# 28 instead of 24 seven-product pairs in a two-layer transformer kernel, with the modulation pieces moved around them

## The chip, the core and the metric

The kernel runs on one core of one Trainium2 chip. A core has TensorE (PE, matrix products into PSUM), VectorE (DVE), ScalarE (ACT), GpSimd (POOL) and SyncE (SP); each works through its own instructions in order, and they wait for each other by semaphores. The metric is the device time of one execution in microseconds (us), lower is better.

## The reference

Two layers over 256 latent and 256 context tokens of width 1024. Each layer has a gated feed-forward part (FFN), a mixer (differential attention, a short gated convolution, a multi-scale pool) and a second FFN; in the second layer that last FFN runs on the latent tokens alone. Every part is normalised, scaled and shifted by modulation vectors, and its result is gated by one:

```python
mod = (silu_c @ w_mod[l] + b_mod[l]).reshape(B, N_MOD, D_MODEL)
mod_c = (silu_cc @ w_mod[l] + b_mod[l]).reshape(1, N_MOD, D_MODEL)
h = h + 0.5 * m[2][:, None] * _swiglu(_modulate(_rms(h, norm_w[l, 0]), m[0], m[1]),
                                      ffn1_w_gu[l], ffn1_w_down[l])
...
y, yc = _hybrid_mixer(u, uc, ctx_out, w_in[l], w_out[l], ...)
h = h + m[5][:, None] * y
h = h + 0.5 * m[8][:, None] * _swiglu(_modulate(_rms(h, norm_w[l, 2]), m[6], m[7]),
                                      ffn2_w_gu[l], ffn2_w_down[l])

def _swiglu(x, w_gu, w_down):
    g, u = jnp.split(x @ w_gu, 2, axis=-1)
    return (jax.nn.silu(g) * u) @ w_down
```

All of it is in float32; the FFN's inner width is 2816.

## The kernel before

**Numbers.** A float32 value is held as a high and a low part, and a product is three matmuls: high x high, high x low, low x high (`three`, lines 1741 to 1743). For the weights ACT makes the high part `whi` (line 575, a "split" below) and DVE the low part `wlo` (line 1023) of each block of 128 x 1024 weights that SP loads into `raw`, a ring of five blocks; SP loads a block when the one five before it is done.

**The FFNs.** They are numbered by `f`: 0 and 1 in the first layer, 2 and 3 in the second; called FFN 0 to FFN 3 below. An FFN has 22 pairs `j` of blocks (gate and up, 256 x 2 token columns) and then two down halves of 11 blocks. A plain pair is 2 x 8 x 3 = 48 matmuls of 512 columns. ACT takes SiLU of the gate (line 588) and DVE multiplies it with up (`hidden`, line 1055).

**Seven-product pairs.** For some pairs (`SEVENS[f]`) the 2 x 2 block product of (gate, up halves) and (token halves) is made with seven products instead of eight: 7 x 4 x 3 = 84 matmuls of 256 columns (`seven_products`). This needs, once per FFN, four sums of the token halves: DVE writes them in pairs 1 and 2 (`x_whole`, `x_sums`: `t32`), ACT makes the high parts `thi` (line 602) and DVE the low parts `tlo` (line 1098, four instructions in pair 3). And it needs, for each such pair, sums of the weight halves: `weight_sums` on DVE (lines 1110 to 1115), `shi` on ACT (line 613), `slo` on DVE (line 1121). PE's order in such a pair: two products of plain parts, then one with `tlo` (it waits for all four), then one that waits for ACT's copy of the pair's first product (`first_copy`, line 622), then three with the weight sums. DVE adds the results up in `seven_begin` (lines 1141, 1145) and `seven_end` (lines 1155, 1157), ACT takes SiLU in two parts (lines 630, 633), `seven_mul` (line 1166) multiplies. `SECOND[f]` names pairs whose weight sums and PSUM banks are a second set; it is empty before.

**Modulation.** The modulation vectors are made beside the FFNs, in 36 units of four pieces (`mod_pair`, line 1041): GpSimd loads a piece of 512 KB into one of two buffers `wm` when the one before is used, and DVE multiplies and accumulates it with the conditioning vector, once per stream (from unit `X_ONLY` = 28 on, for the latent tokens alone). `UNIT_AT[f]` says which units an FFN makes, `MODS_GU[f]` how many pieces stand in each pair, ahead of that pair's `hidden`, and `MODS_DN[f]` how many in each down block.

The order on each engine is that of the code, written out by hand: these tables set it. The functions that the change touches:

Of the kernel before, what the change touches and what calls it, by code (L numbers as in the profile page):

```python
# [64 lines left out]
PAIRS = DC // 2  # L65
# [57 lines left out]
def program(nc, wstream, wmod, cols, x_t, out):  # L123
    with ExitStack() as ctx:
# [394 lines left out]
        def _(pool):  # L519
# [37 lines left out]
            loads(u0 // 2 + 1, after_mix)  # L557
            zeros(0)
            conv_pool_low(0)
            loads(after_mix, UNITS * PAIRS // 2)  # L560
            zeros(1)
            conv_pool_low(1)


        @block.scalar
        def _(act):
# [212 lines left out]
            def mixer(l):  # L779
# [229 lines left out]
        def _(dve):  # L1009
# [21 lines left out]
            def mod_pair(u, p, junk=products):  # L1031
# [337 lines left out]
            def ffn_last():  # L1369
# [1004 lines left out]
```

## Time and profile before

| | us |
|---|---|
| median of 3 runs | 1620.0 (1619.54 to 1620.85) |
| profiled execution, its time | 1619.6 |
| profiled execution, its span | 1617.9 |
| FFN 1, pairs 4 to 20 of its gate/up part | 628 to 806 of the span |
| FFN 2, pairs 4 to 20 | 985 to 1163 |
| FFN 3 | 1404 to 1615 |

All times below are microseconds from the span's start. In the rows, a line of a timeline has start, duration (from the first start to the last end where instructions are merged, x2), engine, line of the code, operation, result<-operands and sizes, and in brackets how long the engine was idle before it and what ended that. Neighbouring instructions overlap by about 0.08 us in these records, so the step from one start to the next is the time one takes in a row of them. The granted clock (PEclk) is the share of TensorE's 2.4 GHz.

### The profile page before, as it was taken

What the parts mean: (1) busy time and instruction counts of PE and PEld (TensorE: products, weight loads), DVE (VectorE), ACT (ScalarE), POOL (GpSimd) and SP (SyncE); (2) the same over time, 40 slices, a digit from 0 to 9 for tenths busy, and PEclk for the clock granted to TensorE, in tenths of its full rate; (3) what the DMA queues carried; (4) which work ended last, traced back from release to release, by engine and by line L of the source; (5) the groups of instructions that cost most, each with busy time, mean ns of one, the idle gap of its engine ahead of it and who ended that gap; (6) DMA issues with size and microseconds to landing.
All of it is one profiled execution on the core that took longest, in us unless ns stands there. A gap on an engine that the chain in (4) does not pass through costs nothing.

```text
span 1617.9 us, 24542 instructions
## 1 busy us (share of the span) xinstructions
PE 1607.8 (99%) x9540; PEld 1407.4 (87%) x9540; DVE 1257.3 (78%) x1926; ACT 697.3 (43%) x1068; POOL 84.6 (5%) x149
## 2 busy tenths in 40 slices
PE   8999999999999999999999999999999999999999
PEld 4889898889878898999988898999988997999888
DVE  5889887888878678788878788888766587887654
ACT  5433233324856454333333154333333275665542
POOL 0000000100000100000000000001000000100000
PEclk9999999999999999999999999999999999999999
DMA  9455554663321223344445434445645332355554
GB/s 378 152 195 176 175 178 149 194 196 105 109 75 53 79 92 118 132 168 156 170 142 189 165 111 133 144 155 200 208 159 205 125 111 82 113 197 182 184 190 148
DMA packets 69615, 250.48 MB, mean 155 GB/s; under 512 B 7552, under 2 KB 8576, under 8 KB 69376
## 3 DMA queue, kind: packets, MB, share of 16 engines
q1 hardware_dynamic: 51072, 181.84, 33.5%
q0 software_dynamic: 18432, 67.12, 11.9%
q8 instruction: 75, 1.23, 0.3%
q14 instruction: 36, 0.29, 0.1%
HBM read 247.88 MB, written 1.05 MB: 154 GB/s over the span
## 4 chain that ended last, share of the span: by engine, by line
PE 95%; DVE 2%; DMA 1%; ACT 1%; issue 0%; DVEq 0%; ACTq 0%
PE ps L1741 28%; PE ps L1742 28%; PE ps L1743 28%; PE ps L1784 3%; PE ps L1832 2%; PE ps L1785 2%; PE ps L1834 1%; PE ps L2153 1%; PE ps L1893 1%; PE ps L2121 1%; DMA raw<-wstream 1%; PE ps L2135 0%; DVE nmax L1548 0%; PE ps L1863 0%; DVE shared_b L1219 0%
## 5 line engine op out<-in xcount | busy, mean ns | idle before, releaser
L1023 DVE TENSOR_TENSOR wlo<-raw,whi 128x1024 fp32r<-128x1024 f32 x320 | 386.6, 1222 | 203.9 <-ACT whi L575 201.3
L1741 PE MATMUL ps<-xh,whi 128*128 128x512 f32 (+1 forms) x1388 | 481.2, 347 | 2.9 <-DVE xl L1227 2.3
L575 ACT ACTIVATE whi<-raw 128x1024 fp32r<-128x1024 f32 x320 | 335.1, 1055 | 341.4 <-PE ps L1743 254.8
L1742 PE MATMUL ps<-xl,whi 128*128 128x512 f32 (+1 forms) x1388 | 473.3, 341 | 0.0
L1743 PE MATMUL ps<-xh,wlo 128*128 128x512 f32 (+1 forms) x1388 | 472.9, 341 | 0.0
L1741 PEld LDWEIGHTS ps<-xh,whi 128*128 128x128 f32 x1388 | 262.8, 189 | 38.9 <-DVE xl L1227 4.4
L1742 PEld LDWEIGHTS ps<-xl,whi 128*128 128x128 f32 x1388 | 263.1, 190 | 29.8 <-issue 0.7
L1743 PEld LDWEIGHTS ps<-xh,wlo 128*128 128x128 f32 x1388 | 262.8, 189 | 30.0
L1742 PE MATMUL ps<-al,whi 128*128 128x512 f32 (+2 forms) x768 | 263.1, 343 | 0.0
L1741 PE MATMUL ps<-ah,whi 128*128 128x512 f32 (+1 forms) x668 | 235.3, 352 | 0.0
L1743 PE MATMUL ps<-ah,wlo 128*128 128x512 f32 (+1 forms) x668 | 234.8, 351 | 0.0
L1742 PEld LDWEIGHTS ps<-al,whi 128*128 128x128 f32 x768 | 145.5, 190 | 17.0
L1741 PEld LDWEIGHTS ps<-ah,whi 128*128 128x128 f32 x668 | 126.2, 189 | 18.1
L1743 PEld LDWEIGHTS ps<-ah,wlo 128*128 128x128 f32 x668 | 126.3, 189 | 16.8
L530 POOL DMA_DIRECT2D wm<-wmod x126 | 66.6, 528 | 991.0 <-DVEq L1045 982.4
L1041 DVE SCALAR_TENSOR_TENSOR wm<-wm,cb 128x1024 f32<-128x1024 f32 x96 | 117.1, 1220 | 0.0
L588 ACT ACTIVATE shared_b<-ps 128x512 f32<-128x512 f32 x42 | 25.1, 598 | 195.5 <-PE ps L1743 195.4
L1041 DVE SCALAR_TENSOR_TENSOR shared_a<-wm,cb 128x1024 f32<-128x1024 f32 x73 | 89.1, 1221 | 11.4 <-DMA wm<-wmod 7.1
L1784 PE MATMUL ps<-xh,whi 128*128 128x512 f32 x208 | 73.5, 399 | 0.0
L1041 DVE SCALAR_TENSOR_TENSOR shared_b<-wm,cb 128x1024 f32<-128x1024 f32 x55 | 67.0, 1218 | 4.8 <-DMA wm<-wmod 4.6
L630 ACT ACTIVATE shared_b<-shared_a 128x256 f32<-128x256 f32 x24 | 10.0, 417 | 135.3 <-DVE shared_a L1141 135.3
L741 ACT ACTIVATE shared_a<-h 128x256 f32<-128x256 f32 (+1 forms) x64 | 31.4, 496 | 66.9 <-DVE h L1177 64.3
(218 smaller groups left out, 2442.6 us busy)
## 6 DMA issues: line engine op xcount, KB each, us to landing
raw<-wstream SPq DMA_DIRECT2D x320, 512.0 KB, 3.5
wm<-wmod POOLq DMA_DIRECT2D x128, 512.0 KB, 4.8
wm<-wmod SPq DMA_DIRECT2D x8, 1024.0 KB, 17.0
h<-x_t SPq DMA_DIRECT2D x4, 512.0 KB, 6.8
cb<-cols SPq DMA_DIRECT2D x1, 1024.0 KB, 19.1
out_t<-h SPq DMA_DIRECT2D x8, 128.0 KB, 2.5
K<-cols SPq DMA_DIRECT2D x1, 907.0 KB, 19.6
K<-cols SPq DMA_DIRECT2D x1, 265.5 KB, 2.9
```

Source lines behind the costliest of these rows:

```text
L530: pool.dma_start(wm[:, c, :, :].rearrange("p a n -> p (a n)"), wmod[bass.ds(i * 2 + c, 1)].rearrange("a p n -> p (a n)"))\
L575: act.activation(whi[:, n % SPL, :, :].rearrange("p a b -> p (a b)"), raw[:, n % RING, :], ACT.Copy)\
L588: act.activation(sil[:, j % 2, 0:w], ps[:, gu_bank(f, 2 * j), 0:w], ACT.Silu).then_inc(silu_done, 1)
L741: act.activation(sq[:, d % 2, a:b], h[:, d, a:b], ACT.Square).then_inc(sq_done, 1)
L1023: dve.tensor_tensor(wlo[:, n % RING, :, :].rearrange("p a b -> p (a b)"), raw[:, n % RING, :], whi[:, n % SPL, :, :].rearrange("p a b -> p ...
L1041: dve.scalar_tensor_tensor(rows if v else junk, rows, 1.0, cb[:, v, :], ALU.mult, ALU.mult, accum_out=flat[:, at:at + 1])\
L1741: pe.matmul(out_ap, hi_w, hi_x, start=start, stop=False)
L1742: pe.matmul(out_ap, hi_w, lo_x, start=False, stop=False)
L1743: return pe.matmul(out_ap, lo_w, hi_x, start=False, stop=stop)
L1784: pe.matmul(ps[:, bank, :], whi[:, n % SPL, c, :], xh[:, c, :], start=c == 0, stop=False)
L1785: return pe.matmul(ps[:, bank, 0:S], wlo[:, n % RING, c, :], xh[:, c, 0:S], start=False, stop=c == DC - 1)
L1832: pe.matmul(ps[:, banks[d], 0:2 * w], hi_w, pair.rearrange("p v t -> p (v t)"), start=start, stop=False)
```

## The change

`SEVENS[1]` and `SEVENS[2]` go from nine to eleven pairs: 4, then runs of two (6 and 7, 9 and 10, 12 and 13, 15 and 16), then 18 and 20. Pairs 7, 10, 13 and 15 use the second set of sums and banks. The modulation pieces of these two FFNs move: one each in pairs 1, 2 and 3, two in the plain pairs 5, 8, 11, 14, 17 and 19, one in 16, 18 and 20. FFN 2 makes 9 units instead of 11; the last two (the gate of FFN 3) are made in FFN 3, one piece per block in the first eight blocks of its first down half, and the gate's columns behind them. GpSimd's loads of those come behind its mixer work. FFN 0 is as it was.

```diff
-UNIT_AT = {0: (4, 12), 1: (16, 9), 2: (25, 11)}
+UNIT_AT = {0: (4, 12), 1: (16, 9), 2: (25, 9), 3: (34, 2)}
...
-          (4, 6, 8, 10, 12, 14, 16, 18, 20),
-          (4, 6, 8, 10, 12, 14, 16, 18, 20))
+          (4, 6, 7, 9, 10, 12, 13, 15, 16, 18, 20),
+          (4, 6, 7, 9, 10, 12, 13, 15, 16, 18, 20))
...
-           {1: 1, 5: 1, 7: 2, 9: 2, 10: 1, 11: 1, 12: 1, 13: 1, 14: 1, 15: 2, 17: 2, 19: 2, 20: 1},
+           {1: 1, 2: 1, 3: 1, 5: 2, 8: 2, 11: 2, 14: 2, 16: 1, 17: 2, 18: 1, 19: 2, 20: 1},
...
-SECOND = ((), (), ())
+SECOND = ((), (7, 10, 13, 15), (7, 10, 13, 15))
...
-            loads(after_mix, UNITS * PAIRS // 2)
+            after_gu = UNIT_AT[3][0] * PAIRS // 2 + 1
+            loads(after_mix, after_gu)
             zeros(1)
             conv_pool_low(1)
+            loads(after_gu, UNITS * PAIRS // 2)
...
-                    act.wait_ge(mod_col, UNITS)
+                    act.wait_ge(mod_col, UNIT_AT[3][0])
...
-                    dve.scalar_tensor_tensor(rows if v else junk, rows, 1.0, cb[:, v, :], ALU.mult, ALU.mult,
+                    dve.scalar_tensor_tensor(junk if u < X_ONLY and v == 0 else rows, rows, 1.0, cb[:, v, :], ALU.mult, ALU.mult,
...
-                gate_columns(m)
...
+                u0, nu = UNIT_AT[f]
                 for b in range(HALF):
                     split_next(nd + b)
+                    if b < nu * PAIRS:
+                        mod_pair(u0 + b // PAIRS, b % PAIRS)
+                mod_columns(u0, nu)
+                gate_columns(m)
```

The table for FFN 2 becomes the same as that for FFN 1. The order that this gives, in the built programs (in the changed one most lines have moved by two):

On DVE, FFN 1, from the last token sums of pair 2 to behind the low parts `tlo` in pair 3 (`hid<-shared_b,ps` is `hidden`, `s` the weight sums, `wlo` a split, `wm` a modulation piece). Before:

```order
L1089 SCALAR_TENSOR_TENSOR t<-t,hid 128x1024
L1092 SCALAR_TENSOR_TENSOR t<-t,hid 128x1024
L1055 TENSOR_TENSOR hid<-shared_b,ps 128x512
L1110 TENSOR_TENSOR s<-raw 128x512
L1111 TENSOR_TENSOR raw<-raw 128x512
L1113 TENSOR_TENSOR s<-s,raw 128x512
L1115 TENSOR_TENSOR s<-s,raw 128x512
L1023 TENSOR_TENSOR wlo<-raw,whi 128x1024 x2
L1121 TENSOR_TENSOR slo<-s,shi 128x1536
L1098 TENSOR_TENSOR tlo<-t,thi 128x1024 x4
L1055 TENSOR_TENSOR hid<-shared_b,ps 128x512
```

and on DVE at the same place now:

```order
L1094 SCALAR_TENSOR_TENSOR t<-t,hid 128x1024
L1043 SCALAR_TENSOR_TENSOR shared_a,modc<-wm,cb 128x1024
L1043 SCALAR_TENSOR_TENSOR wm,modc<-wm,cb 128x1024
L1057 TENSOR_TENSOR hid<-shared_b,ps 128x512
L1112 TENSOR_TENSOR s<-raw 128x512
L1113 TENSOR_TENSOR raw<-raw 128x512
L1115 TENSOR_TENSOR s<-s,raw 128x512
L1117 TENSOR_TENSOR s<-s,raw 128x512
L1025 TENSOR_TENSOR wlo<-raw,whi 128x1024 x2
L1123 TENSOR_TENSOR slo<-s,shi 128x1536
L1100 TENSOR_TENSOR tlo<-t,thi 128x1024 x4
L1043 SCALAR_TENSOR_TENSOR shared_a,modc<-wm,cb 128x1024
```

A piece (two instructions) now stands ahead of pair 2's `hidden`, and one more behind `tlo`.

On ACT, FFN 1, a seven-product pair and the one behind it (`shared_b<-ps 128x256` is the first copy, the two lines `128x2x128` the SiLU parts, `whi` a split, `shi` the sums). Before, pairs 4 to 6:

```order
L622 ACTIVATE shared_b<-ps 128x256
L630 ACTIVATE shared_b<-shared_a 128x2x128
L633 ACTIVATE shared_b<-shared_b 128x2x128
L575 ACTIVATE whi<-raw 128x1024 x2
L613 ACTIVATE shi<-s 128x1536
L588 ACTIVATE shared_b<-ps 128x512
L575 ACTIVATE whi<-raw 128x1024 x2
L622 ACTIVATE shared_b<-ps 128x256
```

and on ACT the run of pairs 6 and 7 now:

```order
L624 ACTIVATE shared_b<-ps 128x256
L577 ACTIVATE whi<-raw 128x1024 x2
L615 ACTIVATE shi_more<-s_more 128x1536
L632 ACTIVATE shared_b<-shared_a 128x2x128
L635 ACTIVATE shared_b<-shared_b 128x2x128
L577 ACTIVATE whi<-raw 128x1024 x2
L624 ACTIVATE shared_b<-ps 128x256
```

The first copy of a run's second pair now stands behind both SiLU parts of the first pair and two splits.

On DVE, the first down half of FFN 3. Before:

```order
L1402 TENSOR_TENSOR shared_b<-shared_b 128x256
L1065 TENSOR_TENSOR ah<-shared_b,ah 128x256
L1023 TENSOR_TENSOR wlo<-raw,whi 128x1024 x11
L1184 SCALAR_TENSOR_TENSOR h<-ps,gcol,h 128x256
L1186 SCALAR_TENSOR_TENSOR h<-ps,gcol,h 128x256
```

and on DVE the end of that half now:

```order
L1025 TENSOR_TENSOR wlo<-raw,whi 128x1024
L1043 SCALAR_TENSOR_TENSOR wm,modc<-wm,cb 128x1024
L1025 TENSOR_TENSOR wlo<-raw,whi 128x1024 x3
L1052 TENSOR_TENSOR modc<-modc,K 128x16
L1173 TENSOR_SCALAR gcol<-modc 128x16
L1186 SCALAR_TENSOR_TENSOR h<-ps,gcol,h 128x256
```

A one-instruction piece stands behind each of the first eight splits, and the gate's columns ahead of the first update.

## Rows read from the trace of the kernel before

**Rows 1.** The page: busy time of each engine.

```profile
PE 1607.8 (99%) x9540; PEld 1407.4 (87%) x9540; DVE 1257.3 (78%) x1926; ACT 697.3 (43%) x1068; POOL 84.6 (5%) x149
```

**Rows 2.** The page: the chain that ended last, by engine.

```profile
PE 95%; DVE 2%; DMA 1%; ACT 1%; issue 0%; DVEq 0%; ACTq 0%
```

**Rows 3.** Waits of PE: us in total, times, longest us.

```profile
PE ps L1741 <- DVE xl L1227: 2.3, 4, 0.6
```

**Rows 4.** Windows, FFN 1: us, PE, PEld, DVE, ACT, POOL busy, PEclk, DMA share, GB/s.

```profile
617.35:628.23 10.88, 10.88 (x49) 9.01 (x48) 10.78 (x12) 7.89 (x8) 0.00 (x0) 1.00 0.30 98
628.23:638.30 10.07, 10.07 (x85) 10.07 (x84) 6.71 (x8) 3.18 (x5) 0.00 (x0) 1.00 0.47 156
638.30:649.21 10.91, 10.91 (x50) 9.02 (x49) 10.35 (x14) 3.92 (x4) 0.00 (x0) 1.00 0.15 50
640.00:915.00 275.00, 275.00 (x1531) 241.42 (x1530) 223.54 (x316) 94.07 (x121) 17.43 (x33) 1.00 0.48 161
```

**Rows 5.** Timeline of DVE, FFN 1, pairs 1 to 3: start, us, what.

```profile
609.60 1.22 DVE L1041 SCALAR_TENSOR_TENSOR shared_a<-wm,cb 128x1024 f32<-128x1024 f32 x1
...
612.47 0.69 DVE L1055 TENSOR_TENSOR hid<-shared_b,ps 128x512 f32<-128x512 f32 x1 [0.50 <-DVE wm L1041]
...
618.88 0.68 DVE L1055 TENSOR_TENSOR hid<-shared_b,ps 128x512 f32<-128x512 f32 x1
619.47 0.68 DVE L1110 TENSOR_TENSOR s<-raw 128x512 f32<-128x512 f32 x1
...
622.12 2.36 DVE L1023 TENSOR_TENSOR wlo<-raw,whi 128x1024 fp32r<-128x1024 f32 x2
624.40 1.75 DVE L1121 TENSOR_TENSOR slo<-s,shi 128x1536 fp32r<-128x1536 f32 x1
626.07 4.62 DVE L1098 TENSOR_TENSOR tlo<-t,thi 128x1024 fp32r<-128x1024 f32 x4
```

**Rows 6.** Timelines: first matmul with the token sums (FFN 1); the same place in FFN 2.

```profile
631.10 0.28 PE L1741 MATMUL ps<-thi,whi 128*128 128x256 f32 x1
...
982.50 4.62 DVE L1098 TENSOR_TENSOR tlo<-t,thi 128x1024 fp32r<-128x1024 f32 x4
...
984.70 0.28 PE L1741 MATMUL ps<-xh,whi 128*128 128x256 f32 x1
```

**Rows 7.** Timeline of DVE, FFN 1, pair 7: two pieces, then the hidden product.

```profile
667.56 1.22 DVE L1041 SCALAR_TENSOR_TENSOR shared_a<-wm,cb 128x1024 f32<-128x1024 f32 x1
...
670.08 1.23 DVE L1041 SCALAR_TENSOR_TENSOR shared_a<-wm,cb 128x1024 f32<-128x1024 f32 x1
...
672.60 0.69 DVE L1055 TENSOR_TENSOR hid<-shared_b,ps 128x512 f32<-128x512 f32 x1
```

**Rows 8.** Timelines of DVE and ACT, FFN 1: sums, SiLU, splits, first copy.

```profile
805.12 0.69 DVE L1141 TENSOR_TENSOR shared_a<-shared_b,ps 128x512 f32<-128x512 f32 x1 [0.25 <-DVE wm L1041]
...
807.02 0.42 ACT L633 ACTIVATE shared_b<-shared_b 128x256 f32<-128x256 f32 x1 [0.70 <-DVE shared_b L1155]
...
670.88 2.00 ACT L575 ACTIVATE whi<-raw 128x1024 fp32r<-128x1024 f32 x2
672.78 0.38 ACT L622 ACTIVATE shared_b<-ps 128x256 f32<-128x256 f32 x1
```

**Rows 9.** FFN 3's first down split on DVE; the page's issue row of the pieces.

```profile
1557.77 1.22 DVE L1023 TENSOR_TENSOR wlo<-raw,whi 128x1024 fp32r<-128x1024 f32 x1 [1.00 <-ACT whi L575]
...
wm<-wmod POOLq DMA_DIRECT2D x128, 512.0 KB, 4.8
```

**Rows 10.** PE's opening groups (3.8 to 8.9, 9.8 to 14.2); windows at the end.

```profile
L1893 PE MATMUL ps<-K 128*128 128x512 f32 x6 | 5.5, 1088 | 3.8 <-DMA K<-cols 3.8
...
L1893 PE MATMUL ps<-K 128*128 128x512 f32 x11 | 4.9, 593 | 0.0
...
1614.85:1616.85 2.00, 0.17 (x2) 0.00 (x0) 0.77 (x2) 0.00 (x0) 0.00 (x0) 1.00 0.64 214
1616.95:1617.90 0.95, 0.00 (x0) 0.00 (x0) 0.00 (x0) 0.00 (x0) 0.00 (x0) 0.50 0.14 45
```

More of the change, by code:

```diff
@@ L83 @@
 SEVENS = ((7, 9, 11, 14, 17, 19),
-          (4, 6, 8, 10, 12, 14, 16, 18, 20),
-          (4, 6, 8, 10, 12, 14, 16, 18, 20))
+          (4, 6, 7, 9, 10, 12, 13, 15, 16, 18, 20),
+          (4, 6, 7, 9, 10, 12, 13, 15, 16, 18, 20))
 MODS_GU = ({2: 1, 3: 1, 4: 2, 5: 2, 6: 2, 8: 2, 9: 1, 10: 2, 11: 1, 12: 2, 13: 2, 14: 1, 15: 2, 16: 2, 18: 2, 19: 2, 20: 2},
-           {1: 1, 5: 1, 7: 2, 9: 2, 10: 1, 11: 1, 12: 1, 13: 1, 14: 1, 15: 2, 17: 2, 19: 2, 20: 1},
-           {1: 1, 5: 1, 6: 1, 7: 2, 9: 2, 11: 2, 12: 1, 13: 2, 14: 2, 15: 2, 16: 2, 17: 2, 18: 2, 19: 2, 20: 2})
+           {1: 1, 2: 1, 3: 1, 5: 2, 8: 2, 11: 2, 14: 2, 16: 1, 17: 2, 18: 1, 19: 2, 20: 1},
+           {1: 1, 2: 1, 3: 1, 5: 2, 8: 2, 11: 2, 14: 2, 16: 1, 17: 2, 18: 1, 19: 2, 20: 1})
 MODS_DN = ({0: 1, 1: 1, 2: 1, 3: 1, 4: 1, 5: 1, 6: 1, 7: 1, 8: 1, 9: 1, 10: 1, 11: 1, 12: 2, 13: 1, 14: 1, 15: 1, 16: 1, 17: 1},
```

## The prediction

> **What bounds the kernel now.** I read the page's busy line first: TensorE (PE) is busy 99% of the span, VectorE (DVE) 78%, ScalarE (ACT) 43% [rows 1]. PE's busy time alone proves little, so the chain of work that ended last comes next: 95% of it is PE [rows 2]. Then who waited for whom on PE: the longest group behind the first load is four waits of at most 0.6 us at stage boundaries [rows 3], and none lies inside the gate/up part of FFN 1 or 2. The windows over single pairs show the same from inside: PE is busy 10.88 of 10.88 us, 10.07 of 10.07, 10.91 of 10.91, and 275.00 of 275.00 over the rest of FFN 1 [rows 4]. So there PE's work is the time: what it loses in work is won, and every wait it gets is paid in full. DVE in the pair before the first seven-product pair is busy 10.78 of 10.88 us [rows 4]: it has no room exactly where that pair's operands are made.
>
> **Part 1, the pairs that become seven-product.** A plain pair is 48 matmuls and lasts 10.88 us, or 10.91 right behind a seven-product pair; a seven-product pair is 84 shorter ones and lasts 10.07 [rows 4]. FFN 1 and FFN 2 go from 9 to 11 such pairs each. Two pairs become shorter: 2 x (10.88 - 10.07) = 1.62 us. The runs of two leave 7 instead of 9 plain pairs behind a seven-product pair: 2 x 0.03 = 0.06. Each FFN gains 1.68 us, the two 3.36. All of it is on the path, because PE waits for nothing there [rows 4].
>
> **Part 2, the piece that moves into pair 2.** A modulation piece is two multiply-accumulates on DVE. One follows the other every 2.52 us (670.08 to 672.60) [rows 7]; once 2.87 us passed (609.60 to 612.47) [rows 5]. Before, pair 1 holds one and pairs 2 to 4 none; now pairs 1, 2 and 3 hold one each. In pair 2 the piece stands ahead of the hidden product, and behind it on DVE stand that product, the weight sums, two splits, the low part of the sums, and the four low parts of the token sums (tlo). In the trace these run without a gap from 618.88 on and tlo ends at 626.07 + 4.62 = 630.69 [rows 5]. The first seven-product pair of FFN 1 starts at 628.23, and its third product, the first that reads tlo, at 631.10 [rows 4, 6]. The slack is 0.41 us, some 0.37 after a handover of about 0.04. A piece more pushes tlo by 2.52: PE would wait 2.52 - 0.37 = 2.15 us. ACT's part moves along, since its sums wait for the same DVE instructions. FFN 2 has the same picture: tlo ends at 982.50 + 4.62 = 987.12, the pair starts at 984.70 and wants tlo 2.88 later, at 987.58; slack 0.42, wait 2.52 - 0.42 + 0.04 = 2.14 [rows 6]. Together +4.28 us. From both sides: nothing, if DVE found a gap to put the piece in, which the rows exclude; 2 x (2.87 - 0.37) = 5.0 with the slow piece. I take 4.28, since nearly all pieces go at 2.52. The piece in pair 3 stands behind tlo and delays only the hidden product of pair 3 (0.6) and the two splits of pair 5 (2.28): 633.2 + 2.52 + 0.6 + 2.28 = 638.6, and PE, itself 2.15 late, reaches pair 5 at 638.30 + 2.15 = 640.45. It costs nothing.
>
> **Part 3, the runs of two.** Here ACT becomes tight. The copy of a pair's first product, for which PE's fourth product waits, now stands in the second pair of a run behind the first pair's second SiLU and two splits. I queue it up from rows. In the trace pair 7 is a plain pair with two pieces, behind a seven-product pair, as the plain pair ahead of a run will be. It starts at 628.23 + 10.07 + 10.91 + 10.07 = 659.28, its pieces at 667.56, its hidden product at 672.60, and DVE is free at 673.2, which is 3.0 us into the next pair (670.19) [rows 4, 7]. In a run of two, DVE then makes the second pair's weight sums (619.47 to 622.12, 2.65), two splits (2.28) and the low part (1.67) [rows 5]: 9.6. From the first sum of the gate to ACT's second SiLU is 805.12 to 807.02, 1.90; that SiLU takes 0.32, two splits 1.90, the copy 0.38 [rows 8]: 14.1 us after the run began, 14.2 with handovers. PE wants it at 10.07 + 3/7 x 10.07 = 14.39. It fits by 0.2 us, in each of the eight runs. I cost it at nothing. If DVE is later than that by more than 0.2, each run pays the excess.
>
> **Part 4, the last gate's units.** FFN 2 loses eight pieces that were hidden there. FFN 3 gets eight, one multiply of 1.2 us each, between the splits of its first down half. There DVE splits a block every 2.8 us, about four blocks ahead of PE (1557.77 for a block that PE reaches some 9 us later) [rows 9]. Two pieces lie ready; six come by DMA, 4.8 us to land [rows 9] plus issue and use, about 7.1 for two, or 21 for six, in the 17 us that PE spends on six blocks. DVE falls back by about 4 of its 9 us. Cost: nothing, unless landing grows beyond some 6.3 us; at 7 about 2 us. On GpSimd's queue the last loads move behind the mixer's work, which has long ended by then. The gate columns (0.2 us) are made on DVE before the sum that needs them.
>
> **Part 5, what the wait does to the clock.** Elsewhere PE waits 0.6 us at most and the granted clock stays at 1.00 (2.4 GHz) [rows 3, 4]. A wait of 2.15 us has no row before the end of the span. There PE is all but idle from 1614.85 on, the clock is still 1.00 up to 1616.85 and reads 0.50 (1.2 GHz) in the last microsecond [rows 10]. So two microseconds of quiet were enough once, and 2.15 us is as long as that. At the lower level PE does half its work: in the opening the first six matmuls took 1088 ns, the later ones 593, and the low stretch was 5.5 us of work [rows 10], so a fall costs between 0 and 2.7 us. I take the middle, 1.4.
> The Trainium skill ("TensorE: Matmul & The Clock Gate", section "HAM oscillation — how this bites in real kernels") says that idle gaps bring PE back to the lower level, but puts the gap that does so above the one worked out here. By that rule the clock holds and the sum is the first rival's 1620.9; the end of this trace speaks against leaning on it.
>
> **The sum.** Against the profiled execution (span 1617.9, time 1619.6): -3.36 + 4.28 = +0.9, and +1.4 for one fall of the clock out of two waits: 1621.9. The median of the runs shown is 1620.0, 0.4 above the profiled one, so for a median **1622.3**. A measurement of this kernel can tell about 0.2% (3.2 us) from no change, so this is "no change": the gain of four pairs goes into two waits for tlo.
>
> **The rivals.** First, the clock holds through both waits: 1620.0 + 0.9 = 1620.9. For it: 1.00 in every earlier stretch; against it: no wait there is as long. Second, on the slower side, the clock falls at both waits and stays low as long as in the opening: 0.9 + 2 x 2.7 = +6.3, 1626.3. It decides for "slower" from (3.2 - 0.9) / 2 = 1.2 us a fall. Third, the runs: with two slow pieces of 2.87 in the plain pair DVE is 0.7 later, the copy comes 0.5 late, eight times: +4.0, 1624.9 with the clock held. Only one such piece is in the rows. Fourth, the wait for tlo doesn't come, because DVE finds the time: 1620.0 - 3.4 = 1616.6, just faster. The missing gap in [rows 5] speaks against it. Fifth, the DMAs of FFN 3 land late: 1620.9 + 2 = 1622.9.
>
> **How the numbers follow.** One fall 0.35, none 0.32, both 0.16, the runs 0.07, no wait 0.06, late DMAs 0.04. Slower by over 0.2% are both falls and the runs, 0.23; faster the fourth rival, 0.06; within 0.2% the rest, 0.71. The range takes in none to two falls and part of the rivals above: low 1619.0 (the clock held, less the scatter of the runs), high 1625.2.
>
> **What would show it.** Right: in PE's waits a new line, DVE tlo, two times, about 2.1 us each, in the first seven-product pair of FFN 1 and FFN 2; tlo ends 2.5 us later against that pair's start; seven-product pairs still 10.07; granted clock below 1.00 right behind one of the two waits. Wrong: no such wait (then 1616.6), waits of PE for ACT's first copy in the runs' second pairs, waits of PE for wlo in FFN 3's down half, or seven-product pairs longer than 10.07.

## The result: no change that counts, by two waits, a clock and one gain not forecast

| | us |
|---|---|
| kernel before, median of 20 runs | 1619.98 (1618.3 to 1621.85) |
| changed kernel, median of 20 runs | 1622.13 (1618.78 to 1626.37) |
| ratio, 95% interval | 1.0018 (1.0012 to 1.0024) |
| changed kernel, profiled execution: time, span | 1625.34, 1623.3 |
| changed kernel, a second profiled execution: span | 1619.5 |

The forecast was 1622.3, in a range of 1619.0 to 1625.2. The median is 2.1 us above the kernel before, where +2.3 was forecast, and the scatter is new: 7.6 us from the lowest run to the highest, against 3.6. That is why two executions of the changed kernel are read below; the first one is 3.2 us above the changed kernel's median, the second near it. In the rows, line numbers of DVE and ACT are 2 higher than before, those of PE 6 higher (in kernels with moved pieces in FFN 3 another 1 to 3).

The page's busy line and its chain, answering to [rows 1, 2]:

```profile
PE 1606.7 (99%) x9684; PEld 1413.9 (87%) x9684; DVE 1284.6 (79%) x1963; ACT 706.5 (44%) x1080; POOL 85.0 (5%) x149
...
PE 89%; DVE 7%; DMA 3%; issue 1%; ACT 1%; DVEq 0%; POOLq 0%; ACTq 0%
```

PE is busy 1.1 us less than before while the span is 5.4 us longer, and 7% of the chain is now DVE: PE has begun to wait. For whom, the waits of PE say (us in total, times, longest us); the last row was there before [rows 3], and so was the load at the start, left out here:

```profile
PE ps L1747 <- DVE tlo L1100: 5.6, 2, 2.8
PE ps L1838 <- DVE wlo L1025: 1.2, 1, 1.2
PE ps L1747 <- DVE xl L1229: 2.3, 4, 0.6
```

The windows over single pairs, answering to [rows 4] (us, PE, PEld, DVE, ACT, POOL busy, PEclk, DMA share, GB/s): pairs 3 and 4 of FFN 1, its run 6 and 7, pair 8, then pair 4 of FFN 2:

```profile
616.57:627.46 10.89, 10.89 (x50) 9.01 (x48) 10.64 (x14) 5.53 (x6) 0.53 (x1) 1.00 0.44 150
627.46:640.52 13.06, 10.29 (x85) 10.12 (x84) 12.18 (x14) 5.42 (x8) 0.53 (x1) 1.00 0.44 152
651.43:671.58 20.15, 20.15 (x169) 20.15 (x168) 16.22 (x21) 7.89 (x11) 1.06 (x2) 1.00 0.52 183
671.58:682.49 10.91, 10.91 (x51) 9.02 (x49) 10.46 (x15) 3.93 (x4) 0.00 (x0) 1.00 0.15 50
...
985.12:1000.83 15.71, 12.90 (x86) 12.72 (x84) 12.33 (x14) 5.47 (x8) 0.53 (x1) 0.78 0.42 134
```

A run of two lasts 20.15, twice 10.07, with PE busy throughout: the new pairs are as short as they should be. The loss of FFN 1 and FFN 2 sits in the two pairs 4, which last 3.0 and 5.6 us longer than a seven-product pair; the second also shows a granted clock of 0.78.

Where the time goes, stage by stage. A stage begins at the same matmul in each kernel: FFN 1 and FFN 2 at the first one behind PE's wait for xl. The other two are cut behind a pair of sums for the norms that stands in every kernel's order (line 1982 before): "mixer 2" begins within FFN 2's last blocks and takes in the first 29 us of FFN 3, "FFN 3" is the rest. The differences to the kernel before add up to that of the span:

| stage | before, us | changed | second execution |
|---|---|---|---|
| start to FFN 1 | 591.90 | -0.76 | -0.81 |
| FFN 1 | 356.49 | +1.18 | +0.84 |
| FFN 2 | 337.99 | +4.00 | +2.32 |
| mixer 2 | 145.13 | -0.85 | -0.76 |
| FFN 3 | 186.39 | +1.83 | +0.01 |
| span | 1617.90 | +5.40 | +1.60 |

FFN 1 and FFN 2 should each be 1.68 shorter for two new pairs; the waits and the clock make them longer. FFN 3's 1.83 holds the wait for wlo, 1.2. The first row is scatter: in the profiles of this study, with either kernel's opening, FFN 1 begins between 590.7 and 592.0. Mixer 2 is a gain that the prediction didn't have.

### The profile page after: what moved, and what is told of

It reads as the page before. It is cut to its first block, busy times and chain, and to the rows that moved or that the text cites. A ratio compares the mean times of both kernels' runs of the same rounds, so it can differ in the third digit from the quotient of the medians.

```text
span 1623.3 us, 24912 instructions
## 1 busy us (share of the span) xinstructions
PE 1606.7 (99%) x9684; PEld 1413.9 (87%) x9684; DVE 1284.6 (79%) x1963; ACT 706.5 (44%) x1080; POOL 85.0 (5%) x149
## 4 chain that ended last, share of the span: by engine, by line
PE 89%; DVE 7%; DMA 3%; issue 1%; ACT 1%; DVEq 0%; POOLq 0%; ACTq 0%
PE ps L1747 27%; PE ps L1748 26%; PE ps L1749 26%; PE ps L1790 3%; PE ps L1791 1%; DMA raw<-wstream 1%; DVE wlo L1025 1%; DMA wm<-wmod 1%; PE ps L2159 1%; DVE wm L1043 1%; PE ps L2127 1%; PE ps L1899 1%; PE ps L1838 1%; DVE tlo L1100 1%; DVE hid L1073 1%
## 5 line engine op out<-in xcount | busy, mean ns | idle before, releaser
L1747 PE MATMUL ps<-xh,whi 128*128 128x512 f32 (+1 forms) x1356 | 465.4, 343 | 2.7 <-DVE xl L1229 2.3
L1748 PE MATMUL ps<-xl,whi 128*128 128x512 f32 (+1 forms) x1356 | 457.5, 337 | 0.0
L1749 PE MATMUL ps<-xh,wlo 128*128 128x512 f32 (+1 forms) x1356 | 457.1, 337 | 0.0
L1747 PEld LDWEIGHTS ps<-xh,whi 128*128 128x128 f32 x1356 | 256.9, 189 | 36.0 <-DVE xl L1229 4.4
L1748 PEld LDWEIGHTS ps<-xl,whi 128*128 128x128 f32 x1356 | 257.1, 190 | 27.3 <-issue 0.7
L1749 PEld LDWEIGHTS ps<-xh,wlo 128*128 128x128 f32 x1356 | 256.9, 189 | 27.5
L1043 DVE SCALAR_TENSOR_TENSOR wm<-wm,cb 128x1024 f32<-128x1024 f32 x128 | 156.2, 1220 | 8.1 <-DMA wm<-wmod 7.4
L1043 DVE SCALAR_TENSOR_TENSOR shared_a<-wm,cb 128x1024 f32<-128x1024 f32 x59 | 72.0, 1221 | 4.1 <-DMA wm<-wmod 1.0
L1747 PE MATMUL ps<-thi,whi 128*128 128x256 f32 x224 | 64.7, 289 | 5.6 <-DVE tlo L1100 5.6
L1749 PE MATMUL ps<-thi,wlo 128*128 128x256 f32 x224 | 64.4, 288 | 0.0
```

The lines of the kernel that those rows point to most:

```text
L1043: dve.scalar_tensor_tensor(junk if u < X_ONLY and v == 0 else rows, rows, 1.0, cb[:, v, :], ALU.mult, ALU.mult, accum_out=flat[:, at:at + 1])\
L1747: pe.matmul(out_ap, hi_w, hi_x, start=start, stop=False)
L1748: pe.matmul(out_ap, hi_w, lo_x, start=False, stop=False)
L1749: return pe.matmul(out_ap, lo_w, hi_x, start=False, stop=stop)
```

## Why the wait is longer than forecast, and why it varies

DVE in pairs 2 to 4 of FFN 1 and PE in pair 4 (timelines: start, us, what), answering to [rows 5, 6]:

```profile
618.76 1.22 DVE L1043 SCALAR_TENSOR_TENSOR shared_a<-wm,cb 128x1024 f32<-128x1024 f32 x1
...
621.28 0.69 DVE L1057 TENSOR_TENSOR hid<-shared_b,ps 128x512 f32<-128x512 f32 x1
...
628.48 4.63 DVE L1100 TENSOR_TENSOR tlo<-t,thi 128x1024 fp32r<-128x1024 f32 x4
...
630.21 0.28 PE L1749 MATMUL ps<-xh,wlo 128*128 128x256 f32 x1
633.25 0.36 PE L1747 MATMUL ps<-thi,whi 128*128 128x256 f32 x1 [2.77 <-DVE tlo L1100]
```

The piece takes the forecast 2.52 us (618.76 to 621.28) and stands where it was expected. But the wait is 2.8, not 2.15. The missing 0.6 was lost 14 us ahead of the piece, when DVE began the sums of x. ACT's split of block 6 and DVE's first sum, in the changed kernel, then the same two in the kernel before:

```profile
602.71 1.06 ACT L577 ACTIVATE whi<-raw 128x1024 fp32r<-128x1024 f32 x1 [1.00 <-DMA raw<-wstream]
604.94 3.49 DVE L1073 TENSOR_TENSOR hid<-xh,xl 128x1024 f32<-128x1024 f32 x3
```

```profile
602.82 1.06 ACT L575 ACTIVATE whi<-raw 128x1024 fp32r<-128x1024 f32 x1 [0.20 <-DMA raw<-wstream]
605.06 1.22 DVE L1071 TENSOR_TENSOR hid<-xh,xl 128x1024 f32<-128x1024 f32 x1
```

PE began block 3 at 600.23 in the changed kernel and at 601.00 before, so DVE's first sum came 4.71 behind that instead of 4.06. Behind it DVE runs nearly without a gap, so the delay d of that first sum decides tlo. In the kernel before, tlo was in time by 0.37 at d = 4.06 in FFN 1, and by 0.38 at d = 4.36 in FFN 2 (where no slow piece stands ahead). So PE's wait should be 2.52 for each piece more in pair 2, plus d, less 4.43 in FFN 1 and less 4.74 in FFN 2. The executions in which PE waited for tlo with at most one piece more and no filler (the kernels are those of the experiments below), with d read as above and the wait from the bracket of PE's row:

| kernel, FFN | pieces more | d, us | wait by the formula | wait measured |
|---|---|---|---|---|
| changed, FFN 1 | 1 | 4.71 | 2.80 | 2.77 |
| changed, FFN 2 | 1 | 5.11 | 2.89 | 2.81 |
| changed, second execution, FFN 1 | 1 | 4.40 | 2.49 | 2.44 |
| changed, second execution, FFN 2 | 1 | 4.53 | 2.31 | 2.23 |
| before with the piece, FFN 1 | 1 | 4.85 | 2.94 | 2.90 |
| before with the piece, FFN 2 | 1 | 4.01 | 1.79 | 1.71 |
| best kernel (last but one below), FFN 2 | 0 | 5.11 | 0.37 | 0.29 |
| FFN 3's pieces spread, FFN 1 | 0 | 4.91 | 0.48 | 0.43 |
| before with FFN 3's pieces, FFN 1 | 0 | 4.66 | 0.23 | 0.19 |

The transfer of block 6 sets d in FFN 1: ACT's wait for it was 0.20 in the kernel before (d 4.06), 0.65 in the second execution (4.40), 1.00 in the first, 1.13 in the kernel before with the piece. It belongs to neither kernel. The prediction had read its slack of 0.37 from one execution, in which block 6 landed early. With two pieces more the formula is 0.3 too high: it gives 4.86 and 5.24, where PE waited 4.24 for tlo in both FFNs and 0.34 and 0.68 for wlo just ahead of the pair.

## What the clock does behind the wait

PE in pair 4 of FFN 2, first execution: the last matmul ahead of the wait, two behind it, one later; then windows of PE (us, busy, PEclk, DMA share, GB/s):

```profile
987.88 0.28 PE L1749 MATMUL ps<-xh,wlo 128*128 128x256 f32 x1
990.96 0.55 PE L1747 MATMUL ps<-thi,whi 128*128 128x256 f32 x1 [2.81 <-DVE tlo L1100]
...
991.74 0.41 PE L1747 MATMUL ps<-thi,whi 128*128 128x256 f32 x1
991.96 0.41 PE L1748 MATMUL ps<-tlo,whi 128*128 128x256 f32 x1
...
997.11 0.28 PE L1749 MATMUL ps<-thi,slo 128*128 128x256 f32 x1
997.23 0.28 PE L1747 MATMUL ps<-thi,shi 128*128 128x256 f32 x1
```

```profile
988.00:991.00 3.00, 0.19 (x3) 0.84 0.60 178
991.00:993.00 2.00, 2.00 (x9) 0.50 0.05 18
...
997.00:999.00 2.00, 2.00 (x19) 1.00 0.65 233
```

Behind the wait a matmul starts every 0.21 us instead of every 0.12, at a granted clock of 0.50 (1.2 GHz), for some 6 us of work; from 997 on it is 1.00 again. The pair lasts 15.71 = 10.07 + 2.97 + 2.67. The 2.97 is the wait of 2.81 and the 0.16 us by which neighbouring matmul records overlap (0.28 long, 0.12 apart), called the refill below; the last term is the clock. Behind the wait of FFN 1, as long as this one, the clock stayed at 1.00. In the second execution it was again FFN 2 alone: the pair lasts 14.02 there, 2.4 of that the wait with its refill and 1.6 the clock. So of the six waits of 1.7 to 2.9 us in the table above two cost the clock, and then 1.6 or 2.7 us. What decides between them is not shown.

The mean granted clock, on record for every execution, tells more than the profiles. It was 1.000 in all 65 executions of the kernel before for which it is listed. The 20 timed executions of the changed kernel:

| mean granted clock | executions | median, us |
|---|---|---|
| 1.000 | 3 | 1620.12 |
| 0.999 | 8 | 1621.75 |
| 0.998 | 8 | 1624.45 |
| 0.997 | 1 | 1626.37 |

So some 17 of 20 executions lost clock (10 of 11 in the second set), and the new scatter goes largely with it.

## The experiments

Four kernels on one chip, then four more, then two, each set timed against the kernel before (median 1619.6 to 1619.9).

**One piece out of pair 2.** In `MODS_GU` and `MODS_DN`, the lines of FFN 1 and FFN 2 (the first 11 entries of a down line are its first half):

```diff
-           {1: 1, 2: 1, 3: 1, 5: 2, 8: 2, 11: 2, 14: 2, 16: 1, 17: 2, 18: 1, 19: 2, 20: 1},
-           {1: 1, 2: 1, 3: 1, 5: 2, 8: 2, 11: 2, 14: 2, 16: 1, 17: 2, 18: 1, 19: 2, 20: 1})
+           {1: 1, 3: 1, 5: 2, 8: 2, 11: 2, 14: 2, 16: 1, 17: 2, 18: 1, 19: 2, 20: 1},
+           {1: 1, 3: 1, 5: 2, 8: 2, 11: 2, 14: 2, 16: 1, 17: 2, 18: 1, 19: 2, 20: 1})
...
-           {0: 1, 1: 1, 2: 1, 3: 1, 4: 1, 5: 1, 6: 1, 7: 1, 8: 1, 9: 1, 10: 1, 11: 1, 12: 1, 13: 1, 14: 1, 15: 1, 16: 1, 17: 1},
-           {0: 1, 1: 1, 2: 1, 3: 1, 4: 1, 5: 1, 6: 1, 7: 1, 8: 1, 9: 1, 10: 1, 11: 1, 12: 1, 13: 1, 14: 1, 15: 1, 16: 1, 17: 1})
+           {0: 1, 1: 1, 2: 1, 3: 1, 4: 1, 5: 1, 6: 1, 7: 1, 8: 1, 9: 1, 10: 1, 11: 1, 12: 2, 13: 1, 14: 1, 15: 1, 16: 1, 17: 1},
+           {0: 1, 1: 1, 2: 1, 3: 1, 4: 1, 5: 1, 6: 1, 7: 1, 8: 1, 9: 1, 10: 1, 11: 1, 12: 2, 13: 1, 14: 1, 15: 1, 16: 1, 17: 1})
```

> The changed kernel with one piece of FFN 1 and of FFN 2 moved from pair 2 to the second down half (block 12, two pieces there instead of one). Theory: the two waits for tlo come from this piece alone, and the fall of the clock from the waits. Both go: no wait of PE for DVE tlo, granted clock 1.00 from the opening to the end, and what stays is the gain of four seven-product pairs (-3.4) and the wait in FFN 3's down half (+1.4): 2.0 us below the kernel before, about 1618.0. Rival: the runs of two, or another operand of the first seven-product pair, come late as well and take the waits' place: a wait of the same place with another releaser, and a time of 1620 or more.

Measured: 1616.94 us, ratio 0.9983 (0.9974 to 0.9992). All that PE waits for behind its first load (waits of PE), and both pairs 4 (windows of PE):

```profile
PE ps L1747 <- DVE xl L1229: 2.3, 4, 0.6
PE ps L1747 <- DVE wlo L1025: 0.3, 1, 0.3
```

```profile
627.40:637.47 10.07, 10.07 (x85) 1.00 0.62 206
982.09:992.30 10.21, 10.21 (x86) 1.00 0.62 203
```

No wait for tlo, no fall of the clock, no other wait in their place: the rival is out. The time is 5.2 us below the changed kernel, and 1.1 lower than expected. The profile is that of the fastest of 11 executions; ten of them have a mean granted clock of 1.000, the slowest (1619.84) has 0.999. The wait in FFN 3 was not there in this profile, although its pieces were unchanged.

**The same, and FFN 3's pieces spread over its gate/up part.**

```diff
+LAST_MODS = (3, 5, 7, 9, 11, 13, 15, 17)
...
                             .then_inc(mul_done, 1)
+                    if j in LAST_MODS:
+                        k = LAST_MODS.index(j)
+                        mod_pair(u0 + k // PAIRS, k % PAIRS)
...
                     split_next(nd + b)
-                    if b < nu * PAIRS:
-                        mod_pair(u0 + b // PAIRS, b % PAIRS)
```

> As the kernel without a piece in pair 2, and FFN 3's eight pieces no longer stand between the splits of its first down half but one each behind pairs 3, 5, 7, ... 17 of its gate/up part, where DVE is idle for about a third of the time. Theory: PE's wait of 1.2 us for wlo in FFN 3's down half comes from wm transfers that land late while the weight stream runs at its fastest; spread over some 90 us it goes, and the whole gain of four seven-product pairs is left: 3.4 us below the kernel before, about 1616.6. Rival: DVE's or the stream's lateness there has another cause (it would be there without pieces): the wait for wlo stays at 1.2 us and the time stays near 1618.0.

Measured: 1615.3, ratio 0.9974 (0.9964 to 0.9983). No wait in the down half, but a new one in FFN 3's gate/up part (waits of PE), beside a small one for tlo with its late weights; then the rows of DVE and PE at the new one:

```profile
PE ps L1749 <- DVE shared_b L1391: 1.1, 1, 1.1
PE ps L1749 <- DVE tlo L1101: 0.4, 1, 0.4
```

```profile
1465.18 1.22 DVE L1044 SCALAR_TENSOR_TENSOR wm<-wm,cb 128x1024 f32<-128x1024 f32 x1
...
1469.54 0.69 DVE L1391 TENSOR_TENSOR shared_b<-ps,shared_b 128x512 f32<-128x512 f32 x1 [0.64 <-ACT srow L709]
...
1470.29 0.39 PE L1749 MATMUL ps<-al,whi 128*128 128x258 f32 x1 [1.07 <-DVE shared_b L1391]
```

PE waits there to begin pair 8, whose banks are free once DVE has scaled pair 6's results (line 1391). The pieces behind pairs 3 and 5 stand ahead of that on DVE, some 2.7 us together, in the pairs (3 to 6) in which DVE still makes the normed input. A place where an engine is idle for a third of the time on average can hold a pair where it isn't. The profiled execution, 1617.3, is 2.0 above the median, so the median may not hold this wait.

**PE kept busy ahead of the wait.** The 20 extra matmuls are read by nobody.

```diff
+                if j == SEVENS[f][0] and f > 0:
+                    for q in range(20):
+                        pe.matmul(ps[:, 7, 0:S].rearrange("p (s t) -> p s t", s=2), whi[:, gate[0], q % KQ, :],
+                                  xh_half[:, q % KQ, :, 0, :], start=True, stop=True)
                 pe.wait_ge(tlo_done, 4 * f + 4)
```

> The changed kernel, and PE makes 20 matmuls of 256 columns more (2.4 us by 0.12 each) into an idle accumulator bank ahead of its wait for tlo in the first seven-product pair of FFN 1 and of FFN 2; nobody reads them. PE is late for tlo by as much as before but not idle for it. Theory: the fall of the granted clock follows from PE's idle time, and costs 2.7 us where it happens, in about half of the waits: the clock stays at 1.00 behind both, what is left of the wait is 0.5 us or less, and the time falls from 1622.1 to about 1620 (1619.5 to 1621). Rival: the clock's fall has another cause, or costs nothing beside the wait: time unchanged at 1622, or above where the matmuls take longer than the wait.

Measured: 1621.02, ratio 1.0007 (0.9998 to 1.0016). Both pairs 4 (windows of PE):

```profile
628.33:641.32 12.99, 12.74 (x106) 1.00 0.48 154
985.92:998.39 12.47, 12.47 (x105) 1.00 0.48 168
```

The clock held behind both, and the mean granted clock is 1.000 in all 11 executions, where the changed kernel had it in 3 of 20: the rival that the fall has another cause than PE's idle time is out. The median is at the upper end of what was expected, 1.1 below the changed kernel's 1622.13, with intervals that overlap. In FFN 2 the filler itself is on the path here: its weights landed early (d 3.91), the wait would have been 1.7, and 20 matmuls take 2.4. So the difference shows less than the clock's full price, and alone it would not settle what a fall costs.

**The kernel before with the piece alone.**

```diff
-           {1: 1, 5: 1, 7: 2, 9: 2, 10: 1, 11: 1, 12: 1, 13: 1, 14: 1, 15: 2, 17: 2, 19: 2, 20: 1},
-           {1: 1, 5: 1, 6: 1, 7: 2, 9: 2, 11: 2, 12: 1, 13: 2, 14: 2, 15: 2, 16: 2, 17: 2, 18: 2, 19: 2, 20: 2})
+           {1: 1, 2: 1, 5: 1, 7: 2, 9: 2, 10: 1, 11: 1, 12: 1, 13: 1, 14: 1, 15: 2, 17: 2, 19: 2},
+           {1: 1, 2: 1, 5: 1, 6: 1, 7: 2, 9: 2, 11: 2, 12: 1, 13: 2, 14: 2, 15: 2, 16: 2, 17: 2, 18: 2, 19: 2, 20: 1})
```

> The kernel before with one change: one piece of FFN 1 and one of FFN 2 move from pair 20 into pair 2. Nothing else of the change. Theory: the piece alone brings the waits for tlo, 2.1 to 2.9 us each, in FFN 1 and FFN 2, and a fall of the clock behind about half of them, 2.7 us: 4.3 to 5.8 for the waits and 0 to 5.4 for the clock, about 7 us above the kernel before, 1627 (1624 to 1630). Rival: the waits belong to the new order of pairs 4 to 7 as well (a run of two right behind), and the piece alone costs 2 us or less.

Measured: 1624.84, ratio 1.0035 (1.0023 to 1.0047): +5.1, inside the expected span and 2 us below its middle. The piece alone makes both waits (waits of PE: 2.9 and 1.7):

```profile
PE ps L1741 <- DVE tlo L1098: 4.6, 2, 2.9
```

The clock stayed at 1.00 in this profile, and the mean is 1.000 in four of the six executions: here the falls were rarer than in the changed kernel, which fits a time below the middle of what was expected. The runs of two have no part in the waits.

**The kernel before with FFN 3's pieces alone.**

```diff
-UNIT_AT = {0: (4, 12), 1: (16, 9), 2: (25, 11)}
+UNIT_AT = {0: (4, 12), 1: (16, 9), 2: (25, 9), 3: (34, 2)}
...
-           {1: 1, 5: 1, 6: 1, 7: 2, 9: 2, 11: 2, 12: 1, 13: 2, 14: 2, 15: 2, 16: 2, 17: 2, 18: 2, 19: 2, 20: 2})
+           {1: 1, 5: 1, 6: 1, 7: 2, 9: 2, 11: 1, 12: 1, 13: 1, 14: 1, 15: 1, 16: 1, 17: 1, 18: 2, 19: 1, 20: 1})
...
```

The rest of the diff is that of the change behind its tables.

> The kernel before with the change's last part alone: FFN 2 loses eight pieces (one each from pairs 11, 13, 14, 15, 16, 17, 19, 20), FFN 3 gets them between the splits of its first down half, with the GpSimd, ScalarE and VectorE edits that belong to it; no new seven-product pair, no piece in pair 2. Theory: PE waits for wlo in FFN 3's down half only in executions in which a wm transfer lands later than some 6.3 us, 1.4 us then: median 0 to +1 us against the kernel before (1620 to 1621). Rival: the late landing and the wait are there in nearly every execution: +1.4 or more in the median. Second rival: the FFN 2 with fewer pieces gains by itself: below the kernel before.

Measured: 1620.63, ratio 1.0008 (0.9999 to 1.0017): +1.0, at the upper end of the theory's span and not to be told from nothing. Its profile shows the wait, 0.8 us. How it comes about is best seen in the first execution of the changed kernel: GpSimd issues a piece, DVE uses it 7.4 us later and splits behind it, PE stands (timelines of POOL, DVE and PE):

```profile
1578.26 0.53 POOL L530 DMA_DIRECT2D wm<-wmod  x1 [3.62 <-DVEq L1047]
...
1585.70 1.23 DVE L1043 SCALAR_TENSOR_TENSOR wm<-wm,cb 128x1024 f32<-128x1024 f32 x1 [3.37 <-DMA wm<-wmod]
1587.08 1.23 DVE L1025 TENSOR_TENSOR wlo<-raw,whi 128x1024 fp32r<-128x1024 f32 x1
...
1588.45 0.47 PE L1838 MATMUL ps<-ah,whi 128*128 128x512 f32 x1 [1.22 <-DVE wlo L1025]
```

The longest landing of the six pieces was 7.4 us there and 6.6 here, with waits of 1.2 and 0.8; it was 6.0, 5.9, 5.4, 5.4 and 5.4 in the five other profiles with these pieces in this place, with no such wait.

**Two pieces in pair 2** of FFN 1 and FFN 2.

```diff
-           {1: 1, 2: 1, 3: 1, 5: 2, 8: 2, 11: 2, 14: 2, 16: 1, 17: 2, 18: 1, 19: 2, 20: 1},
-           {1: 1, 2: 1, 3: 1, 5: 2, 8: 2, 11: 2, 14: 2, 16: 1, 17: 2, 18: 1, 19: 2, 20: 1})
+           {1: 1, 2: 2, 5: 2, 8: 2, 11: 2, 14: 2, 16: 1, 17: 2, 18: 1, 19: 2, 20: 1},
+           {1: 1, 2: 2, 5: 2, 8: 2, 11: 2, 14: 2, 16: 1, 17: 2, 18: 1, 19: 2, 20: 1})
```

> The changed kernel with two pieces in pair 2 of FFN 1 and FFN 2, pair 3's having moved there. Theory: tlo is 2.52 us later again, PE waits 4.7 to 5.4 us twice, and behind a wait of that length the clock falls nearly every time, 2.7 us each, where one piece made it fall about every second time: +5.0 for the waits and +1 to +3 for the clock on top of the changed kernel's 1622.1, 1628 to 1630. Rival: the clock's fall has nothing to do with the length of the wait: +5.0 alone, 1627.1.

Measured: 1629.42, ratio 1.006 (1.0047 to 1.0074), as expected; the rival's 1627.1 lies below all five executions. Their mean granted clock is 0.996 or 0.997: more was lost than with one piece.

**Two pieces, and 42 unread matmuls ahead of the wait.** The diff is that of the 20, with `range(42)`.

> The same with two pieces in pair 2, and PE makes 42 unread matmuls of 256 columns (5.0 us) ahead of each wait for tlo. Theory: the path is as long as with two pieces, but PE isn't idle, so the clock stays at 1.00 and the difference between the two kernels is the clock alone: 2 to 5.4 us less, about 1626 to 1627. Rival: the clock costs nothing of its own (PE would wait for VectorE anyway): no difference between the two.

Measured: 1627.62, ratio 1.0047 (1.0033 to 1.006). Both pairs 4 in windows of PE, first with two pieces, then with the filler:

```profile
628.29:644.40 16.11, 11.87 (x85) 0.89 0.30 98
989.84:1006.43 16.59, 12.35 (x85) 0.79 0.30 95
```

```profile
629.49:644.67 15.18, 15.18 (x126) 1.00 0.30 103
989.28:1004.43 15.15, 15.15 (x128) 1.00 0.34 108
```

With two pieces PE waits 4.24 us twice and the clock falls behind both; with the filler it holds behind both. The filler makes the path longer than the wait did: a pair with wait and refill would last 10.07 + 4.39 = 14.46, and these last 15.18 and 15.15, together 1.4 more. (In both profiles PE also waits 1.0 to 1.1 us for wlo just ahead of these pairs, so that doesn't part them.) So the two falls cost 1.8 + 1.4 = 3.2 us between the medians, and 16.11 + 16.59 - 2 x 14.46 = 3.8 in the profile. The rival that the clock costs nothing of its own is out; by all profiles a fall costs between 1.6 and 2.7.

**No piece in pairs 1 and 2 of FFN 1 and FFN 2, FFN 3's pieces in pairs 7 to 20.** The loop over `LAST_MODS` is that of the second kernel.

```diff
+LAST_MODS = (7, 9, 11, 13, 15, 17, 19, 20)
...
-           {1: 1, 2: 1, 3: 1, 5: 2, 8: 2, 11: 2, 14: 2, 16: 1, 17: 2, 18: 1, 19: 2, 20: 1},
-           {1: 1, 2: 1, 3: 1, 5: 2, 8: 2, 11: 2, 14: 2, 16: 1, 17: 2, 18: 1, 19: 2, 20: 1})
+           {3: 1, 5: 2, 8: 2, 11: 2, 14: 2, 16: 1, 17: 2, 18: 1, 19: 2, 20: 1},
+           {3: 1, 5: 2, 8: 2, 11: 2, 14: 2, 16: 1, 17: 2, 18: 1, 19: 2, 20: 1})
...
-           {0: 1, 1: 1, 2: 1, 3: 1, 4: 1, 5: 1, 6: 1, 7: 1, 8: 1, 9: 1, 10: 1, 11: 1, 12: 1, 13: 1, 14: 1, 15: 1, 16: 1, 17: 1},
-           {0: 1, 1: 1, 2: 1, 3: 1, 4: 1, 5: 1, 6: 1, 7: 1, 8: 1, 9: 1, 10: 1, 11: 1, 12: 1, 13: 1, 14: 1, 15: 1, 16: 1, 17: 1})
+           {0: 1, 1: 1, 2: 1, 3: 1, 4: 1, 5: 1, 6: 1, 7: 1, 8: 1, 9: 1, 10: 1, 11: 1, 12: 2, 13: 1, 14: 2, 15: 1, 16: 1, 17: 1},
+           {0: 1, 1: 1, 2: 1, 3: 1, 4: 1, 5: 1, 6: 1, 7: 1, 8: 1, 9: 1, 10: 1, 11: 1, 12: 2, 13: 1, 14: 2, 15: 1, 16: 1, 17: 1})
```

> The changed kernel with no piece in pairs 1 and 2 of FFN 1 and FFN 2 (both moved to the second down half, blocks 12 and 14, two there), and FFN 3's eight pieces behind pairs 7, 9, 11, 13, 15, 17, 19 and 20 of its gate/up part, clear of the pairs in which VectorE still makes the normed input. Theory: what the two kernels with moved pieces still lost (0.1 to 0.7 us for tlo where the weights land late at an FFN's start, 1.1 us for the gate's scaled sums in FFN 3's pair 3) goes as well: 4.5 to 5 us below the kernel before, about 1615.0, with less scatter upwards. Rival: what is left is not these waits, and the pieces only move the lateness elsewhere (wlo in the second down half): 1616 or more.

Measured: 1616.2, ratio 0.9978 (0.9969 to 0.9987). No wait for tlo and none in FFN 3, but a new one at the end of FFN 1's second down half, where DVE waited 1.60 us for a piece's transfer (waits of PE):

```profile
PE ps L1749 <- DVE h L1180: 0.4, 1, 0.4
PE ps L1990 <- DVE shared_a L1204: 0.2, 1, 0.2
```

So the rival holds in part: here two more pieces, nine in the seven blocks of that half that take any, were too many. One of FFN 2's runs of two also lasted 20.35 instead of 20.15 in this profile.

**Pair 1 keeps its piece, FFN 3's stand in pairs 7 to 20.** The tables of the first experiment, with `LAST_MODS` of the kernel above.

> The changed kernel with no piece in pair 2 of FFN 1 and FFN 2 (one more at block 12 of the second down half, pair 1 keeps its own), and FFN 3's eight pieces behind pairs 7 to 20 of its gate/up part. Theory: the wait of 1.1 us in FFN 3's pair 3 (with the piece that stood there) goes, no wait at the end of the second down half appears (that needed a second moved piece), and PE waits for tlo 0.1 to 0.7 us at most, where the weights land late at an FFN's start: about 1615.0 to 1615.5, 4.5 us below the kernel before. Rival: FFN 3's pieces are no cost in the median at either place, and the time stays where the kernel without a piece in pair 2 was, 1617.

Measured: 1615.01, ratio 0.9973 (0.9962 to 0.9984), as expected. It is the best of the kernels here, 4.9 us below the kernel before and 6.6 below the changed one timed beside it, though the interval doesn't part it from the three others without a piece in pair 2. In its profile FFN 1 is 1.81 shorter than before, FFN 2 1.12 and mixer 2 0.91; 1.19 is FFN 1's earlier begin, which is scatter. What PE still waits for beyond xl (waits of PE):

```profile
PE ps L1749 <- DVE tlo L1101: 0.3, 1, 0.3
PE ps L1749 <- DVE wlo L1026: 0.3, 1, 0.3
```

**The changed kernel again.** No edit.

> The changed kernel again, unaltered, for a second profile of it. Theory: PE is late for tlo by 2.15 us plus what VectorE's first sums of x begin later than 4.06 us after the FFN's start (0 to 0.9 us, by the landing of the weights of blocks 5 and 6), so 2.1 to 3.0 us in each of FFN 1 and FFN 2, and the clock falls behind neither, one or both; a wait for wlo in FFN 3's down half only if a wm transfer there lands later than 6.3 us. Rival: both waits are 2.8 us and more whatever the landing, and the wait in FFN 3 is there every time. Time 1622, as before.

Measured: 1621.57, ratio 1.0017 (1.0008 to 1.0026). The waits go by the landing (2.44 and 2.23, in the table above), and FFN 3 has none: the theory's two points held, the rival's didn't. (What the expectation calls the FFN's start is PE's start of block 3, as for d above.)

## The prediction, part by part

**Part 1, four pairs for 3.36 us: right.** A run of two lasts 20.15, and without the waits FFN 1 is 1.81 shorter (one piece out of pair 2; 1.68 forecast).

**Part 2, the piece in pair 2: right in place and mechanism, too small.** Forecast were 2.15 and 2.14 us of wait; the two executions show 2.77 and 2.81, 2.44 and 2.23. The step that failed is the slack: 0.37 us read from one execution, taken as a constant of the kernel, while the landing of the weights moves it by about 1 us. By the same reading it is negative (-0.2 to -0.5) at one of the two FFNs in three of the five profiles with pair 1's piece alone, which are the small waits for tlo of 0.2 to 0.4 there. The bound of 5.0 for both waits came near the measured 5.6 and 4.7 for a wrong reason (a slow piece).

**Part 3, the runs of two: right, with hardly any margin.** The second pair's copy, forecast to end 14.1 us after the run began and wanted at 14.39, ends at 665.16 + 0.36 = 665.52 in the run from 651.43 on (14.09), by this row of ACT's timeline, answering to [rows 8]:

```profile
665.16 0.36 ACT L624 ACTIVATE shared_b<-ps 128x256 f32<-128x256 f32 x1
```

Of the 72 runs of two in the nine profiles with the new pairs, 71 lasted 20.15, with that copy ending 14.08 to 14.11 behind the run's begin. In one, in the kernel without pieces in pairs 1 and 2, DVE had begun its pieces 0.35 later; the copy ended at 14.44 and the run lasted 20.35. So the queue that was forecast is real, and a margin of 0.3 was just enough.

**Part 4, FFN 3's pieces: right as a rule, wrong as a certainty.** "Nothing, unless landing grows beyond some 6.3 us" is what seven profiles show: waits at 6.6 and 7.4, none up to 6.0. But it happened in two of seven, and the fifth rival had a chance of 0.04. The price was lower than forecast: 1.2 at 7.4 us, where about 2 was expected at 7. The landing of 4.8 us was a median over all pieces; in this stretch pieces and weight stream move 259 GB/s together (1560 to 1600) against 184 in the gate/up part ahead.

**Part 5, the clock: right in kind, its share too small.** One fall in two waits, 1.4 us, was forecast; both executions of the changed kernel show one fall, at 2.7 and 1.6. But "none" had a chance of 0.32, and 3 of 20 executions lost no clock; their median, 1620.12, is 2.0 below that of all. That a wait of this length sometimes costs the clock and sometimes not is what was argued from the end of the trace. The Trainium skill's rule, cited in the prediction ("TensorE: Matmul & The Clock Gate", section "HAM oscillation — how this bites in real kernels"), would have had the clock hold behind waits as short as these; FFN 2's 2.81 and 2.23 us speak against it.

**What the sum lacked.** Mixer 2 is 0.76 to 1.02 shorter in eight of the nine profiles with the new pairs in FFN 2 and 0.28 in the ninth; in the two profiles of variants of the kernel before it is 0.05 and 0.37. In the first execution 0.47 of it comes where PE reads the squares of the heads, 41 us into that stage, and most of the rest where it takes up FFN 3's first normed input. Why was not tried and stays open. With it the second execution closes: -3.36 + 4.99 (waits with refill) + 1.57 (clock) - 0.76 (mixer 2) - 0.81 (start) = 1.63, against 1.60 measured. That the forecast of the median came out within 0.2 us is partly luck: the waits and the clock cost more than forecast, and this gain stood against them.

**The rivals.** "The clock holds" and "both fall" are the lower and upper part of the new scatter rather than cases apart; the runs' late copy was seen in one run of 72, never in the changed kernel's two profiles; "no wait for tlo" is out; the late DMAs happen in some executions.

## To carry to other kernels

A slack read from one profile is one draw: look for what stands at the head of the chain (here a transfer, some 27 us before the wait) and ask how late it can be before a piece of 2.5 us is put into 0.4 us of room. Of one change its good part can be had alone: with the runs of two the kernel was 4.9 us faster as soon as each piece stood where VectorE had room, pair by pair rather than on the average of a stage (3.4 were forecast for the pairs). Where PE will wait as long as here, count the clock as well, about 2 us for each time it falls. Filling the wait with unread matmuls held the clock each time; it costs what they exceed the wait by, and still won 1.8 us where that was 0.7 twice.

## What the runs showed of the hardware

- The granted clock fell behind 2 of 6 waits of PE of 1.7 to 2.9 us and behind 2 of 2 of 4.2 us, and behind none that was filled with matmuls. The mean granted clock was 1.000 in all 16 executions with a filler, in 4 of 31 of the changed kernel and in none of 5 with two pieces. Behind a fall a 256-column matmul took 0.21 us instead of 0.12.
- Two waits of the same length (2.77 and 2.81 us) in one execution differed in this: one cost nothing more, the other 2.7 us.
- A weight block's landing at an FFN's start differed by about 1 us between executions (ACT waited 0.20 to 1.13 us for the same block), and a 512 KB piece beside the weight stream of FFN 3's down half landed in 3.8 to 7.4 us.
- In the profile of the kernel before with the piece alone, FFN 3 was 1.6 us shorter than in any other one without a wait there; its matmuls went at 117 per 20 us against 115 in the kernel before. It was not followed up, and that kernel is judged by its median.
